# Last scan of a hybrid conformer/SSD layer: order of the stored outputs, of the decode step, and of the second operand's conversion

## The reference, cut to what matters

```python
y, new_h = ssd_scan(xs, dt, a_neg, bm, cm, ssm_h)      # per group: 4 heads, 256 channels
y = y + xs * ssm_d[:, None]
y = y.reshape(b, l, D_INNER) * jax.nn.silu(z)
y = rmsnorm(y.reshape(b, l, N_GROUPS, D_INNER // N_GROUPS), ...)   # norm inside each group
branch_b = y @ ssm_w_out                                # 2048 -> 1024
merged = sigmoid(gate_a) * branch_a + sigmoid(gate_b) * branch_b
```

## Time and profile before

| what | us |
|---|---|
| median of 3 executions | 1276.14 (1276.02 to 1276.47) |
| the profiled execution, its own time | 1276.54 |
| its span in the trace | 1274.8 |
| TensorE busy with matmuls | 1212.6 (95% of the span) |
| VectorE busy | 807.4 (63%) |
| ScalarE busy | 642.7 (50%) |
| GpSimd busy | 130.7 (10%) |
| granted TensorE clock, mean of the core | 0.983 of full |

### The profile page before, as it was taken

How to read it: one execution, slowest core, us unless ns; L and a number is a source line. 1 busy time by engine, 2 the same in 40 slices (tenths; PEclk the granted TensorE clock), 3 DMA queues, 4 the chain that set the end, 5 groups by cost and what they waited for, 6 DMA issues and landing times.

```text
span 1274.8 us, 22805 instructions
## 1 busy us (share of the span) xinstructions
PE 1212.6 (95%) x9582; PEld 1187.3 (93%) x9582; DVE 807.4 (63%) x1058; ACT 642.7 (50%) x1284; POOL 130.7 (10%) x228
## 2 busy tenths in 40 slices
PE   3999999999999999999779699999999999999995
PEld 2998999999999999999769699999999999999995
DVE  6756888889788888878667656654433433432443
ACT  5446665766667486675554555535412422422432
POOL 1110120302103030120300100000000000000000
PEclk9998999999999999999979899999999999999998
DMA  4461382735537364463633513442221221221201
GB/s 162 146 207 49 115 252 75 221 118 150 196 110 224 114 188 158 114 233 107 197 140 123 213 49 137 171 143 76 100 100 67 100 100 66 99 94 71 99 33 70
DMA packets 31077, 165.25 MB, mean 130 GB/s; under 512 B 4352, under 2 KB 4480, under 8 KB 17680
## 3 DMA queue, kind: packets, MB, share of 16 engines
q1 hardware_dynamic: 14832, 97.52, 21.5%
q0 software_dynamic: 16160, 66.52, 17.1%
HBM read 131.23 MB, written 23.87 MB: 122 GB/s over the span
## 4 chain that ended last, share of the span: by engine, by line
PE 87%; ACT 2%; DMA 1%; issue 1%; DVE 1%; POOL 0%; DVEq 0%; ACTq 0%; POOLq 0%
PE main L567 70%; PE main L588 8%; PE py L660 2%; PE py L641 1%; PE ph L648 1%; PE py L646 1%; PE pt L629 1%; DMA arena<-y_scratch 1%; DMA y_scratch<-dec 1%; PE ps L630 1%; PE ps L698 0%; PE ph L677 0%; DVE arena L1698 0%; ACT w_hi L846 0%; PE pt L670 0%
## 5 line engine op out<-in xcount | busy, mean ns | idle before, releaser
L567 PE MATMUL main<-ra_hi,w_hi 128*128 128x272 f32 x1984 | 585.4, 295 | 17.1 <-DVE ra_lo L1532 15.3
L567 PE MATMUL main<-ra_hi,w_lo 128*128 128x272 f32 x1984 | 576.3, 290 | 0.0
L567 PE MATMUL main<-ra_lo,w_hi 128*128 128x272 f32 x1984 | 571.9, 288 | 0.0
L567 PEld LDWEIGHTS main<-ra_hi,w_hi 128*128 128x128 f32 x1984 | 375.7, 189 | 18.1 <-issue 16.2
L567 PEld LDWEIGHTS main<-ra_lo,w_hi 128*128 128x128 f32 x1984 | 376.0, 190 | 0.2
L567 PEld LDWEIGHTS main<-ra_hi,w_lo 128*128 128x128 f32 x1984 | 374.6, 189 | 0.0
L1217 DVE TENSOR_TENSOR w_lo<-w_raw,w_hi 128x2048 fp32r<-128x2048 f32 x88 | 201.4, 2289 | 67.4 <-ACT w_hi L846 67.4
L846 ACT ACTIVATE w_hi<-w_raw 128x2048 fp32r<-128x2048 f32 x88 | 168.0, 1910 | 113.0 <-PE main L567 91.4
L567 PE MATMUL main<-rb_hi,w_lo 128*128 128x272 f32 x576 | 166.8, 290 | 0.0
L567 PE MATMUL main<-rb_hi,w_hi 128*128 128x272 f32 x576 | 166.1, 288 | 0.4 <-DVE arena L1569 0.4
L567 PE MATMUL main<-rb_lo,w_hi 128*128 128x272 f32 x576 | 165.6, 288 | 0.0
(11 more groups left out here) (281 smaller groups left out, 1564.0 us busy)
## 6 DMA issues: line engine op xcount, KB each, us to landing
w_raw<-in_w_all SPq DMA_DIRECT2D x88, 1024.0 KB, 4.9
dec<-mask_f POOLq DMA_DIRECT2D x8, 1088.0 KB, 5.0
dec<-acum_scratch POOLq DMA_DIRECT2D x16, 544.0 KB, 8.4
dec<-in_ssm_state POOLq DMA_DIRECT2D x8, 1024.0 KB, 6.2
out_hs<-dec POOLq DMA_DIRECT2D x8, 1024.0 KB, 8.6
dec<-acum_scratch POOLq DMA_DIRECT2D x16, 272.0 KB, 4.1
gate_scratch<-arena POOLq DMA_DIRECT2D x16, 272.0 KB, 6.9
arena<-gate_scratch POOLq DMA_DIRECT2D x8, 544.0 KB, 3.9
```

The lines of the kernel that those rows point to most:

```text
L567: last = pe.matmul(psum[t % 2][:, hf, 0:H2], w[:, bs, at:at + P], x[:, k, hf * H2:(hf + 1) * H2], start=(k == 0 and j == 0), stop=(k == KT ...
```

## The change

- GpSimd, g = 7: the wait on `sil_ready` and the four loads of y_ld0 stand ahead of `save_conf_state`, `store_states(6)`, `store_yn(6)`, the wait for both and `load_states(7)`.
- GpSimd, after the loop: `store_states(7)` stands ahead of the waits and of the loads of xc.
- TensorE: in the last scan `decode_stat` is issued behind `decode_end`, after tile (3, 0) in place of (3, 1).
- The operand rb is laid out by `Y_TILE`: the k-th K tile lies in tile 4, 5, 6, 7, 1, 2, 0, 3 of rb. `fill` takes it with the argument `tile`. Block 44 is two plain `fill`s; the first waits per k in the first column half.
- ScalarE: six `y_high` (k = 0 to 5) stand between `hi_of(44)` and `y_rstd`, with `b_out(6)` after the fourth; two are left behind the norm.
- VectorE: `conv.finish` stands ahead of `decode_m`; four `y_low` stand ahead of `decode_norm`, four behind the wait for `st_st`.

```diff
--- before.py
+++ after.py
@@ -176,6 +176,8 @@
         ps = ctx.enter_context(nc.psum_tensor("ps", [P, 512], F32))
         py = ctx.enter_context(nc.psum_tensor("py", [P, 512], F32))
         ph = ctx.enter_context(nc.psum_tensor("ph", [P, 512], F32))
+
+        Y_TILE = (4, 5, 6, 7, 1, 2, 0, 3)
 
         def main(t):
             return psum[t % 2][:, :, 0:H2]
@@ -507,16 +509,16 @@
                 conf_prefix(g)
                 if g + 1 < GROUPS:
                     load_conf_state(g + 1)
+                if g == GROUPS - 1:
+                    pool.wait_ge(sil_ready, 4 * GROUPS)
+                    for q in range(4):
+                        pool.dma_start(y_ld0[:, 2 * q:2 * q + 2, :], y_dram[q]).then_inc(y_in, 16)
                 save_conf_state(g)
                 store_states(p)
                 store_yn(p)
                 pool.wait_ge(st_st, 16 * g)
                 pool.wait_ge(yn_st, 16 * g)
                 load_states(g)
-                if g == GROUPS - 1:
-                    pool.wait_ge(sil_ready, 4 * GROUPS)
-                    for q in range(4):
-                        pool.dma_start(y_ld0[:, 2 * q:2 * q + 2, :], y_dram[q]).then_inc(y_in, 16)
                 store_gates(g)
 
             p = GROUPS - 1
@@ -524,6 +526,7 @@
             for q in range(3):
                 pool.dma_start(y_ld1[:, 2 * q:2 * q + 2, :], y_dram[4 + q]).then_inc(y_in, 16)
             add_cc(p)
+            store_states(p)
             for s_out in (ssd_st, cc_st, cout_st, sout_st):
                 pool.wait_ge(s_out, 16 * GROUPS)
             for m in range(2):
@@ -531,7 +534,6 @@
             for i in range(2):
                 pool.dma_start(xc[:, 4 * i:4 * i + 4, :], cc_dram[4 * i:4 * i + 4].rearrange("a p n -> p a n"))\
                     .then_inc(cc_in, 16)
-            store_states(p)
 
             pool.wait_ge(ys_ready, 3 * KT)
             for m in range(KT):
@@ -547,7 +549,7 @@
 
         @block.tensor
         def _(pe):
-            def fill(b, rhs_hi, rhs_lo, t0, m0=0, m1=2, between=None, half=None):
+            def fill(b, rhs_hi, rhs_lo, t0, m0=0, m1=2, between=None, half=None, tile=range(KT)):
 
                 bs, be, count = b
                 for m in range(m0, m1):
@@ -565,7 +567,7 @@
                             at = k * BW + m * P
                             for j, (w, x) in enumerate(((w_hi, rhs_hi), (w_hi, rhs_lo), (w_lo, rhs_hi))):
                                 last = pe.matmul(psum[t % 2][:, hf, 0:H2], w[:, bs, at:at + P],
-                                                 x[:, k, hf * H2:(hf + 1) * H2],
+                                                 x[:, tile[k], hf * H2:(hf + 1) * H2],
                                                  start=(k == 0 and j == 0), stop=(k == KT - 1 and j == 2))
                     last.then_inc(tile_done, 1)
 
@@ -709,7 +711,7 @@
 
                 return spread_off
 
-            def after_tile(j, m, p):
+            def after_tile(j, m, p, soon=False):
 
                 if j < 2:
                     c = 2 * j + m
@@ -722,7 +724,9 @@
                     decode_mid(p)
                 elif (j, m) == (3, 0):
                     decode_end(p)
-                elif (j, m) == (3, 1):
+                    if soon:
+                        decode_stat(p)
+                elif (j, m) == (3, 1) and not soon:
                     decode_stat(p)
 
             def group(g, ssd):
@@ -775,7 +779,7 @@
 
                     fill(blk(j % 2, B_SSM + j), ra_hi, ra_lo, 0, m, m + 1,
                          between=y_arrives if (j, m) == (0, 0) else off if (j, m) == (2, 0) else None)
-                    after_tile(j, m, p)
+                    after_tile(j, m, p, soon=True)
 
             pe.wait_ge(cc_added, GROUPS)
             pe.wait_ge(d_ycur, GROUPS)
@@ -783,8 +787,13 @@
             pe.matmul(py[:, :], ones[:, :], cc_sum[:, 0:SEQ], start=True, stop=True)
             pe.matmul(ph[:, 0:NDEC], ones[:, :], cc_sum[:, SEQ:T], start=True, stop=True).then_inc(l_stat, 1)
 
-            fill_late(blk(0, B_SSM + 4), rb_hi, rb_lo, ys_ready, 2 * KT)
-            fill(blk(1, B_SSM + 5), rb_hi, rb_lo, 0)
+            def y_follows(n):
+                if n < KT:
+                    pe.wait_ge(ys_ready, 2 * KT + n + 1)
+
+            fill(blk(0, B_SSM + 4), rb_hi, rb_lo, 0, 0, 1, between=y_follows, tile=Y_TILE)
+            fill(blk(0, B_SSM + 4), rb_hi, rb_lo, 0, 1, 2, tile=Y_TILE)
+            fill(blk(1, B_SSM + 5), rb_hi, rb_lo, 0, tile=Y_TILE)
             pe.wait_ge(d_rstd_s, GROUPS)
             pe.wait_ge(l_ssum_s, KT)
             for hf, bank in enumerate((pt, ps)):
@@ -792,7 +801,7 @@
                                  start=True, stop=True)
             last.then_inc(l_stat2, 1)
             for i in range(2, 4):
-                fill(blk(i % 2, B_SSM + 4 + i), rb_hi, rb_lo, 0)
+                fill(blk(i % 2, B_SSM + 4 + i), rb_hi, rb_lo, 0, tile=Y_TILE)
 
             fill_late(blk(0, B_PW), ra_hi, ra_lo, cc_split, 0)
             for i in range(1, 4):
@@ -1087,14 +1096,16 @@
             b_out(5)
             y_square(p)
             hi_of(B_SSM + 4)
-            b_out(6)
+            act.wait_ge(y_in, 16 * 7)
+            for k in range(6):
+                y_high(Y_TILE[k], slice(0, T), y_ld1[:, k, :], rb_hi)
+                if k == 3:
+                    b_out(6)
             y_rstd(p)
             b_out(7)
-
-            act.wait_ge(y_in, 16 * 7)
             act.wait_ge(d_yn_s, GROUPS)
-            for k in range(KT):
-                y_high(k, slice(0, T), y_ld1[:, k, :] if k < 6 else y_sb[:, k - 6, :], rb_hi)
+            for k in range(6, KT):
+                y_high(Y_TILE[k], slice(0, T), y_sb[:, k - 6, :], rb_hi)
             hi_of(B_SSM + 5)
             act.wait_ge(l_stat, 1)
             act.activation(l_mean[:, 0:SEQ], py[:, :], ACT.Copy, scale=1.0 / D_MODEL)
@@ -1539,17 +1550,20 @@
             p = GROUPS - 1
             chunks(p, conv, B_SSM + 1, B_SSM + 2)
             lo_of(B_SSM + 3)
+            conv.finish()
             n_st = decode_m(p, conv)
-            conv.finish()
             decode_y(p, n_st)
             decode_sum(p)
             lo_of(B_SSM + 4)
             decode_last(p)
+            dve.wait_ge(d_ycur, GROUPS)
+            dve.wait_ge(d_ssum_s, GROUPS)
+            for k in range(4):
+                y_low(Y_TILE[k], slice(0, T), y_ld1[:, k, :], rb_hi, rb_lo, 2 * KT + k)
             decode_norm(p)
-
             dve.wait_ge(st_st, 16 * GROUPS)
-            for k in range(KT):
-                y_low(k, slice(0, T), y_ld1[:, k, :] if k < 6 else y_sb[:, k - 6, :], rb_hi, rb_lo, 2 * KT + k)
+            for k in range(4, KT):
+                y_low(Y_TILE[k], slice(0, T), y_ld1[:, k, :] if k < 6 else y_sb[:, k - 6, :], rb_hi, rb_lo, 2 * KT + k)
             lo_of(B_SSM + 5)
 
             def square_sum(m):
```

## The result

The changed kernel takes 1254.74 us (median of 4 executions, 1254.19 to 1255.23) against 1276.31 us for the kernel before on the same chip (4 executions, 1276.02 to 1276.63): ratio 0.9831, 95% interval 0.9814 to 0.9848. It won 21.6 us; 26.5 were forecast, and 1254.7 lies inside the range of 1246 to 1256, near its slow end. The profiled execution took 1255.23 us with a span of 1253.5.

What follows compares the result with a forecast made beforehand. TensorE bounds the kernel, busy 1212.6 of 1274.8 us, so only its gaps in blocks 40 and 44 can be won. Terms -16.5 and -10.0 sum to -26.5 us, giving 1249.6 us; range 1246.0 to 1256.0.

Steps and rivals of the forecast that it cites:

- The two places: TensorE's gaps of 15.3 us in block 40 and 9.9 us in block 44, at most 30.3 us with clock losses.
- my own case: Whole kernel: both terms come as worked out, 1249.6 us, within 1247 to 1252.5; 73 in 100.
- the second rival: Blocks 40 and 44: transfers share and don't queue, so both landings come later, 1255 to 1259 us; 8 in 100.
- signs by which I said I would be wrong: Block 40 still waits over 4 us, `y_low` waits for the norm, or `b_add(1)` makes TensorE wait in block 45.
- Part 1: Block 40: y_ld0's loads go first, landing at 630.7, so `ssd_2` of chunk 1 starts 16.5 us earlier.
- Same company, later: y_ld0's landing in block 40: again 10.29 us from first issue with 1 MB beside it, 631.15 at the late side.
- The new waits in `ssd_2`: Block 40 at full clock: TensorE waits 0.4 us for `ssd_x` and 0.45 us for the scores of chunk 1.
- Part 2: End of the scan: block 44's gap nearly closes and it is done at 727.25, not 737.26; -10.0 us.
- The rule on the shared port: GpSimd's addition locks out VectorE operations with two SBUF inputs: delay at the new place at most 1.16 us, hidden.
- The rule on completion counts: Store before block 44: counts follow a DMA engine's earlier writes, so xc loads now behind couldn't hold up its landing.
- The clock rival for block 44: The clock falls in block 44's thin stretch: 2.2 us lost, 1251.8; with the first restart too, 1254.5; 13 in 100.
- The norm as the next limit: Block 44: rival dependence such as the norm as late as the store, 1259.6, 4 in 100; forecast 712.7 against landing 715.

Runs made afterwards that it cites:

- the two halves alone: Kernel before with only y_ld0's loads moved: 1264.56 us; changed kernel with that move undone: 1264.06 us; both against 1275.55 for the kernel before.
- the early loads: Changed kernel with y_ld0's four loads issued still earlier, right behind load_decay(7), ahead of add_cc(6): 1250.23 us, ratio 0.9802 to the kernel before.
- the late sums: Changed kernel with decode_stat put back behind tile (3, 1): 1257.01 us, ratio 0.9853 to the kernel before.
- the one with only the store cut: Changed kernel with only the store of group 7's states cut, first 6 of 8 sequences, then the rest: 1252.30 us, ratio 0.9821 to before.

## Why the prediction was right, and where its sum was off

**The two places and their mechanisms: right.** The second gap closed, and the first shrank from 15.3 to 4.1 us, for the reasons given, independently (the two halves alone), and nothing behind M2 changed. But the time lies outside the 1247 to 1252.5 of my own case (73 in 100): it is inside the range only since the high end had been put at 1256 for rivals, and the first half of the second rival, shared transfers and a lost clock at block 40 (1249.6 + 3.1 + 2.6 = 1255.3), is about what happened. One of the signs by which I said I would be wrong was met, though barely: block 40 still waited over 4 us, 4.07 in the changed kernel's trace and 3.7 to 4.7 in the five others with the same loads.

**Part 1, mis-sized: -16.5 forecast, -11.75 measured.** The issue of the loads was right to 0.15 us (622.39 against 620.86 + 1.38 for the later start). The step that failed is "Same company, later: 620.86 + 10.29 = 631.15 is the late side", with 630.7 taken: the landing came 13.0 us after the first issue, at 634.0 by before's time. I had counted one megabyte of company. The trace has two and a half: in the 13.0 us 4.7 MB moved, 2.2 of them the loads. The runs put numbers to it: 2.4 us for the weights of block 42, 1.2 for the part of the stores that came in. With both held back it was 9.7 us, and that this is the forecast 9.8 (630.7 - 620.86) is luck: the 9.8 had a megabyte of company in it, and without company the forecast was 7.6 (628.5 - 620.86). Even then 0.7 MB went beside the loads (0.29 MB of it in SyncE's queue, the rest of block 41's weights; the others are `cc`, issued at 618.4, and `out_conf`), and the mean rate was 305 GB/s and not the 396 of rows 3. I had the case as a rival, at 633.8, with 8 in 100, for transfers that "share, they don't queue". The landing was right there (633.8 against 634.0); after the fact the chance looks too small.

**The clock at block 40: not in my own case.** At a forecast wait of 0.8 us none was to be lost. At 4.1 us the tile took 8.42 in place of 6.04 us. So of the 4.75 us missing, 3.3 are the landing (634.0 - 630.7) and the rest the lower clock, net of the two new waits that the slower tile hid again.

**The new waits in `ssd_2`: right where they could show.** In the changed kernel the slow tile hides them. With the early loads (1250.23) they are there, 0.36 us for ScalarE's `ssd_x` and 0.32 for the scores; forecast were 0.4 and 0.45.

**What the loads were moved past: right, less cover than said.** `load_states(7)` went out at 640.13 (forecast 636 + 1.4), and still nobody waited.

**Part 2: -10.0 forecast, -10.9 measured.** The chain was met step by step. Store issued 43.4 us after `ssd_2` of chunk 1, as forecast (706.45 - 663.02 against 696.07 - 652.66). It landed in 7.6 us, not 8.6, and that is about the 0.9 us. `conv.finish` ended 0.96 us ahead of the first operation of `decode_m`, `decode_y` was not delayed, `decode_stat` waited for nothing. The rule on the shared port that the prediction takes from the Trainium skill ("SBUF — State Buffer", section "SBUF: two separate sides") told the size of the moved delay from above: 0.94 us at L1414, under the 1.16 us of the addition, hidden. The row of 1.82 us, of which I had said that it agrees, agrees only in kind: its delay of 1.4 us is longer than the one addition, and no run shows what the other 0.25 us are. The rule on completion counts from the Trainium skill ("DMA: Bandwidth & Descriptors", section "Queues, rings and completion order") had the xc loads as the cause of before's slow landing; putting them ahead again changed stretch 2 by 0.05 us, but in that run they are issued 8 us ahead of the store and not 5, so it neither bears the rule out nor speaks against it.

**The clock rival for block 44: did not happen, and could have.** The clock stayed at 1.00 in the changed kernel and even with a wait of 2.4 us (the late sums), but fell in the kernel with `conv.finish` late, at 1.9 us. So it was a real rival; whether 13 in 100 was the right chance, one kernel can't say.

**The norm as the next limit: right in order, closer than it looked.** `decode_norm` is done 1.7 us ahead of the store's landing (2.3 in the forecast, 712.7 against 715); the 2.3 us that the late sums cost show it.

## What to carry to other kernels

When a load is moved earlier, its landing is worked out from all that the DMA engines have to move in the new place, other queues included, and the share and GB/s of that stretch say how much; then ask whether the company can wait, since holding back one megabyte that nobody needed yet won 3.7 us, about as much as issuing the loads 10 us earlier did (3.0 and 4.9 in two executions). A TensorE gap also costs the clock: going from a wait of 4.1 us to 1.7 won 3.7 us, and that belongs in the price. And when one limit goes, the next is near: here the norm was ready only 1.7 us ahead of the store, so undoing one of the edits gave back 2.3 or 4.2 of the 10.9 us.

## What the runs showed of the hardware that was not expected

- Bytes beside a load cost it the same from either queue, within the scatter of single traces: about 0.9 MB in SyncE's queue 2.4 us, about 0.6 MB of stores on GpSimd's own queue 1.2 us. Of 1.5 MB of stores issued behind the loads on the same queue that much still moved before the loads had landed.
- While two accumulating broadcasts were in flight the DMA share was 0.85 to 1.17 and only 139 to 163 GB/s moved; from 620 us on a share near 1 moved 317 to 435 in the stretches shown. A share near 1 does not tell how many bytes move.
- The clock fell 2.0 to 5.3 us after a gap in block 40 began (2.0 in the changed kernel, 4.2 in before, 5.3 in the one with only the store cut), even where TensorE had worked again for over a microsecond by then (gap of 2.9 us), but not after gaps of 1.7 and 2.4 us in block 40; in block 44 it fell with a wait of 1.9 us and held with one of 2.4. The length of the last gap alone does not tell it.
- The time ahead of M0, with the same instructions, varied from 106.3 to 109.1 us between kernels.
